# A hybrid decoder layer in one kernel: gate columns evacuated later, four reordered starts, and the keys of the recurrence turned by VectorE from stored squares

## What is computed

```python
xn = rms_norm(x, g_norm);  proj = xn @ w_in
(q, k, v, o_pre, z_ml, i_pre, f_pre, b_g, c_g, xc, z_cv, q_x, z_x) = split_in(proj)
# mLSTM, 4 heads of 256, chunk by chunk (shortened: F, m_t, w_inter, w_C, w_s from the gates)
S = einsum('bthd,bshd->bhts', qb, kb) * exp(Dm - m_t)
num = w_inter * einsum('bthd,bhde->bhte', qb, C) + einsum('bhts,bshe->bhte', S, vb)
C_new = w_C * C + einsum('bhs,bshd,bshe->bhde', w_s, kb, vb)
y_ml = head_norm(sigmoid(o_pre) * num / den) * silu(z_ml)
y_cv = b_g * conv3(c_g * xc) * silu(z_cv)
y_xa = softmax(q_x @ mem_k / sqrt(128)) @ mem_v * silu(z_x)
y = concat([y_ml, y_cv, y_xa]) @ w_out;  out = rms_norm(x + y, g_final)
```

## Time and profile before

| | |
|---|---|
| three runs | 2092.15, 2092.35, 2095.11 us, median 2092.35 |
| the profiled execution | 2096.34 us, its span 2094.5 us |
| PE busy | 2058.3 us, 98% of the span |
| DVE, ACT, POOL busy | 67%, 44%, 42% |
| granted clock of TensorE, mean | 0.992 |
| moved by DMA | 312.00 MB, mean 149 GB/s |

### The profile page before, as it was taken

How to read it: one execution, slowest core, us unless ns; L and a number is a source line. 1 busy time by engine, 2 the same in 40 slices (tenths; PEclk the granted TensorE clock), 3 DMA queues, 4 the chain that set the end, 5 groups by cost and what they waited for, 6 DMA issues and landing times.

```text
span 2094.5 us, 34395 instructions
## 1 busy us (share of the span) xinstructions
PE 2058.3 (98%) x12463; PEld 1914.8 (91%) x12463; DVE 1401.5 (67%) x2189; ACT 928.2 (44%) x1900; POOL 884.0 (42%) x728
## 2 busy tenths in 40 slices
PE   8899999999999999999999999999999999999998
PEld 5899999999999999999999999988887878888886
DVE  7567776698767766797777766643435457667774
ACT  5454445545444455454454455433334323333331
POOL 2455555575555555665555555411000122222220
PEclk9999999999999999999999999999999999999999
DMA  6544334555443345455434465565437577777755
GB/s 217 126 125 126 120 112 132 137 129 130 134 120 114 123 139 139 110 139 128 126 115 126 123 133 148 153 203 184 134 111 212 175 217 205 205 206 210 209 155 112
DMA packets 449768, 312.00 MB, mean 149 GB/s; under 512 B 182976, under 2 KB 414272, under 8 KB 449600
## 3 DMA queue, kind: packets, MB, share of 16 engines
q1 hardware_dynamic: 443920, 291.05, 49.8%
q10 hardware_dynamic: 3376, 10.36, 1.3%
q0 software_dynamic: 2304, 8.39, 1.1%
HBM read 224.82 MB, written 84.92 MB: 148 GB/s over the span
## 4 chain that ended last, share of the span: by engine, by line
PE 93%; SPq 2%; DVE 1%; DMA 1%; issue 1%; ACT 1%; ACTq 0%; DVEq 0%; POOLq 0%; POOL 0%
PE bank L695 20%; PE bank L697 20%; PE bank L696 20%; PE bank L2236 3%; PE bank L2238 3%; PE bank L2237 3%; PE bank L2203 3%; PE bank L2190 2%; PE bank L1649 1%; PE bank L1651 1%; PE bank L1650 1%; PE bank L1661 1%; PE bank L763 1%; PE bank L1663 1%; PE bank L1662 1%
## 5 line engine op out<-in xcount | busy, mean ns | idle before, releaser
L695 PE MATMUL bank<-xh,wh 128*128 128x352 f32 x2688 | 870.8, 324 | 9.4 <-ACT snap L878 8.0
L697 PE MATMUL bank<-xh,wl 128*128 128x352 f32 x2688 | 865.2, 322 | 0.0
L696 PE MATMUL bank<-xl,wh 128*128 128x352 f32 x2688 | 863.4, 321 | 0.0
L1081 DVE TENSOR_TENSOR wl<-raw,wh 128x512 fp32r<-128x512 f32 x384 | 421.8, 1100 | 202.5 <-ACT wh L843 201.4
L695 PEld LDWEIGHTS bank<-xh,wh 128*128 128x128 f32 x2688 | 505.0, 188 | 13.3 <-ACT snap L878 8.9
L696 PEld LDWEIGHTS bank<-xl,wh 128*128 128x128 f32 x2688 | 506.5, 188 | 0.3 <-issue 0.2
L697 PEld LDWEIGHTS bank<-xh,wl 128*128 128x128 f32 x2688 | 506.5, 188 | 0.0
L878 ACT ACTIVATE snap<-bank 128x352 f32<-128x352 f32 x384 | 178.4, 465 | 377.1 <-PE bank L697 377.0
L1081 DVE TENSOR_TENSOR wl<-wt,wh 128x512 fp32r<-128x512 f32 x288 | 236.2, 824 | 115.2 <-ACT wh L843 114.4
L843 ACT ACTIVATE wh<-raw 128x512 fp32r<-128x512 f32 x384 | 240.4, 628 | 156.3 <-PE bank L697 154.8
L643 POOL TENSOR_TENSOR stage<-snap 128x352 f32<-128x352 f32 x96 | 96.4, 1004 | 462.0 <-ACT snap L878 460.8
(11 more groups left out here) (339 smaller groups left out, 2641.7 us busy)
## 6 DMA issues: line engine op xcount, KB each, us to landing
raw<-in_w_in SPq DMA_DIRECT2D x72, 1024.0 KB, 5.5
raw<-in_w_in SPq DMA_DIRECT2D x48, 512.0 KB, 5.5
scr_qk<-stage SPq DMA_DIRECT2D x48, 352.0 KB, 6.2
raw<-scr_qk SPq DMA_DIRECT2D x16, 1024.0 KB, 7.3
area<-scr_vob SPq DMA_DIRECT2D x32, 512.0 KB, 7.1
scr_vob<-stage SPq DMA_DIRECT2D x128, 88.0 KB, 3.2
scr_z<-stage SPq DMA_DIRECT2D x24, 352.0 KB, 2.2
scr_xa<-stage SPq DMA_DIRECT2D x24, 352.0 KB, 2.5
```

Of the source, the lines that this page charges most:

```text
L695: pe.matmul(out, wh[:, b, k, :], xh[:, b, k, :], start=(first and k == 0), stop=False, skip_group_check=True)
L696: pe.matmul(out, wh[:, b, k, :], xl[:, b, k, :], start=False, stop=False, skip_group_check=True)
L697: m = pe.matmul(out, wl[:, b, k, :], xh[:, b, k, :], start=False, stop=(k == 3), skip_group_check=True)
L1081: dve.tensor_tensor(low, source(q, b), high.bitcast(F32), ALU.subtract).then_inc(S["w_low"], 1)
```

## The change

Five edits.

1. **Gate columns.** The evacuation of `bank[6]` leaves its place between two `w_high` and becomes `gates_back(q)`, behind all seven `w_high` of the next job. The four stores to `scr_gate` move from ACT's queue to SP's.
2. **Start of attend.** `out_conv(0)` is cut into its two column halves. PE does half 0, `turn_p(0)`, `scores(1)`, then half 1, `weigh_values(0)`.
3. **q and k of tiles 0 and 1.** Their two loads move from t = 10 to t = 14 of attend.
4. **Start of recur.** `values` is divided into `values` (v) and `out_gates` (o). v and the keys of tile 2 are loaded before `load_unit(1)`, o and `gf` behind it.
5. **Keys.** The four k jobs of a pass also store their rows as squares (eight more DMAs a job). From tile 2 on, SP loads these squares (`key_squares`, 512 KB a tile) into a new tile `kb`, VectorE turns them in one instruction 128x1024 (`turn_keys` of VectorE, in front of update 7 of the tile before), and ACT scales them in place. `kw` has two buffers. PE turns keys only for tiles 0 and 1.

```diff
 def store_parts(s, kind, i):
+    if kind == "qk":
+        return 1 if i < 4 else 5
...
         def store(q):
...
+            if JOBS[q][1] == "gate":
+                s = JOBS[q][0]
+                sp.wait_ge(S["gate_evacuated"], s + 1)
+                for j in range(4):
...
+                    sp.dma_start(w["gate"][...], gst[32 * j:32 * j + 8, :]).then_inc(S["gate_out"], 16)
+                return
...
+                if kind == "qk" and JOBS[q][2] >= 4:
+                    store_squares(sp, q, n, S[f"stored{p}{n}"])
...
+        def gates_back(q):
+            s, kind, _ = JOBS[q]
+            if kind == "gate":
+                act.wait_ge(S["gates_summed"], s + 1)
+                wait(act, S["post"], CN.posted[q][0])
+                if s == 0:
+                    act.wait_ge(S["kv_stored"], 80)
+                    act.wait_ge(S["bif_loaded"], 32)
+                act.activation(gst, bank[6][:, 0:HALF], ACT.Identity, bias=bif[:, 0:1]).then_inc(S["gate_evacuated"], 1)
...
-            if t == WM_FIRST:
+            if t == WM_FIRST + KM // 2:
...
-        out_conv(0)
+        out_conv(0, (0,))
...
         turn_p(0)
         scores(1)
+        out_conv(0, (1,))
...
+        def key_squares(t):
+            if SQUARES_FROM <= t < NT:
+                wait(sp, S["keys_turned"], t - SQUARES_FROM)
+                load_squares(sp, w, 2, kb[:, :], t, S["kb_loaded"])
...
             if t:
                 values(t + 2)
+                key_squares(t + 2)
+                out_gates(t + 2)
...
         def scores(t):
             p = t % 2
             wait(pe, S["C_updated"], updates_before(t))
+            if t >= 2:
+                pe.wait_ge(S[f"qk_loaded{p}"], 16 * (t // 2))
...
+                if d == 0:
+                    pe.wait_ge(S["kw_ready"], 4 * t + h + 1)
+                m = pe.matmul(out, kw[t % 2][:, h, d * P:(d + 1) * P], v1[t % 2][:, h, :], start=True, stop=True)
...
             if t + 1 < NT:
-                turn_keys(t + 1)
+                if t + 1 < SQUARES_FROM:
+                    turn_keys(t + 1)
                 scores(t + 1)
...
+            if t >= SQUARES_FROM:
+                act.wait_ge(S["keys_turned"], t - SQUARES_FROM + 1)
+                for h in range(H):
+                    act.activation(kw[t % 2][:, h, :], kw[t % 2][:, h, :], ACT.Copy, scale=wsc[:, h, t:t + 1]).then_inc(S["kw_ready"], 1)
+                return
...
+        def turn_keys(t):
+            if not SQUARES_FROM <= t < NT:
+                return
+            dve.wait_ge(S["kb_loaded"], 16 * (t - SQUARES_FROM + 1))
+            dve.wait_ge(S["dC_summed"], updates_before(t - 2) + 8)
+            dve.transpose(kw[t % 2], kb[:, :].rearrange("p (h d) -> p h d", h=H)).then_inc(S["keys_turned"], 1)
...
                 update(t, j)
                 if j in (1, 3):
                     turn_v(t + 1, j // 2)
+                if j == 6:
+                    turn_keys(t + 1)
```

More of the change, by code:

```diff
@@ L270, in __init__ @@
             for n in stored_rows(kind):
-                stores[p][n] += 16 * store_parts(s, kind)
+                stores[p][n] += 16 * store_parts(s, kind, i)
             self.posted.append(tuple(posts))
@@ L402, in store_squares @@
         s, kind, i = JOBS[q]
-        f, made = 2 * i + n, stage[:, CN.pair[q] % 2, n, :]
+        f, made = 2 * (i % 4) + n, stage[:, CN.pair[q] % 2, n, :]
         groups = (min(T, PASS * (s + 1)) - PASS * s) // SQ
-        to = w["vob"][int(kind == "o"), PASS // SQ * s:PASS // SQ * s + groups]
+        to = w["vob"][("v", "o", "qk").index(kind), PASS // SQ * s:PASS // SQ * s + groups]
         for b in range(4):
@@ L408, in store_squares @@
                          made[SQ * b:SQ * (b + 1), 0:SQ * groups].rearrange("p (g j) -> p g j", j=SQ)).then_inc(sem, 16)
-        if s == PASSES - 1:
+        if s == PASSES - 1 and kind != "qk":
             sp.dma_start(w["vo"][8 * (kind == "o") + f], made[:, SQ * groups:PASS]).then_inc(sem, 16)
@@ L470, in store @@
         def store(q):
-            if q < 0 or JOBS[q][1] == "gate":
+            if q < 0:
+                return
[3 more added lines that the diff above has]
+                for j in range(4):
+                    at = PASS * s + HALF * (j // 2)
+                    sp.dma_start(w["gate"][8 * (j % 2):8 * (j % 2) + 8, at:at + HALF],
+                                 gst[32 * j:32 * j + 8, :]).then_inc(S["gate_out"], 16)
                 return
@@ L853, in evacuate @@
         def evacuate(q, i):
-            s, kind, _ = JOBS[q]
-            if kind == "gate":
-                if i == 2:
-                    act.wait_ge(S["gates_summed"], s + 1)
-                    wait(act, S["post"], CN.posted[q][0])
-                    if s == 0:
-                        act.wait_ge(S["kv_stored"], 80)
-                        act.wait_ge(S["bif_loaded"], 32)
-                    act.activation(gst, bank[6][:, 0:HALF], ACT.Identity, bias=bif[:, 0:1]).then_inc(S["gate_evacuated"], 1)
-                    act.wait_ge(S["gate_evacuated"], s + 1)
-                    for j in range(4):
-                        at = PASS * s + HALF * (j // 2)
-                        act.dma_start(w["gate"][8 * (j % 2):8 * (j % 2) + 8, at:at + HALF],
-                                      gst[32 * j:32 * j + 8, :]).then_inc(S["gate_out"], 16)
+            if JOBS[q][1] == "gate":
                 return
@@ L1640, in turn_k, with out_conv @@
             s_turned[0] += 1
-        def out_conv(t):
+        def out_conv(t, halves=(0, 1)):
             pe.wait_ge(S["cv_split"], t + 1)
             for k in range(4):
-                for n in range(2):
+                for n in halves:
                     if k == 0:
@@ L1651, in out_conv @@
                     m = pe.matmul(out, yl[:, k, :], wxh[k][:, c], start=False, stop=False)
-            m.then_inc(S["cv_used"], 1)
+            if halves[-1]:
+                m.then_inc(S["cv_used"], 1)
         def out_xa(t):
@@ L1922, in recur @@
     UNIT_LOADS = 12
+    SQUARES_FROM = 2
     qk = qk_tiles(raw)
@@ L1927, in recur @@
     qs = wide[:, 1024:2048].rearrange("p (f t) -> p f t", f=8)
-    kw = wide[:, 2048:3072].rearrange("p (h d) -> p h d", h=H)
+    kw = [a.rearrange("p (h d) -> p h d", h=H) for a in (wide[:, 2048:3072], overlay(22560, "m_kw1", [P, D])[:, :])]
+    kb = overlay(18464, "m_kb", [P, D])
     C = wide[:, 3072:5128].rearrange("p (h d e) -> p h d e", h=H, d=2)
@@ L2047, in _ @@
         values(1)
+        out_gates(1)
         load_unit(sp, 0, rest=False)
@@ L2050, in _ @@
         early(2)
+        values(2)
         sp.wait_ge(before["out_summed"], LAST_X)
+        key_squares(2)
+        load_unit(sp, 1)
+        out_gates(2)
         sp.dma_start(gf[:, :], row_bcast(g_final, P)).then_inc(S["gf_loaded"], 16)
-        load_unit(sp, 1)
-        values(2)
         sp.wait_ge(before["res_added"], LAST_X)
@@ L2180, in numerators @@
                 pe.wait_ge(S["ones"], 2)
+            if t >= SQUARES_FROM:
+                pe.wait_ge(S["t1_ready"], 4 * t)
+                pe.wait_ge(S["den_ready"], t)
+                wait(pe, S["s_C_updated"], 4 * units_before(t))
             for h in range(H):
                 if h < 2:
-                    pe.wait_ge(S["kw_ready"], 4 * t + 2 * h + 2)
+                    if t < SQUARES_FROM:
+                        pe.wait_ge(S["kw_ready"], 4 * t + 2 * h + 2)
                 else:
@@ L2375, in keys @@
                 return
-            wait(act, S["dC_summed"], updates_before(t - 1) + 8 if t else 0)
+            if t >= SQUARES_FROM:
+                act.wait_ge(S["keys_turned"], t - SQUARES_FROM + 1)
+                for h in range(H):
+                    act.activation(kw[t % 2][:, h, :], kw[t % 2][:, h, :], ACT.Copy, scale=wsc[:, h, t:t + 1]).then_inc(S["kw_ready"], 1)
+                return
+            if t:
+                act.wait_ge(before["out_summed"], LAST_X)
             for h in range(H):
                 act.wait_ge(S["k_turned"], 2 * t + h // 2 + 1)
-                act.activation(kw[:, h, :], bank[1 + h // 2][:, (h % 2) * HD:(h % 2 + 1) * HD], ACT.Copy,
+                act.activation(kw[t % 2][:, h, :], bank[1 + h // 2][:, (h % 2) * HD:(h % 2 + 1) * HD], ACT.Copy,
                                scale=wsc[:, h, t:t + 1]).then_inc(S["kw_ready"], 1)
```

10 lines of the change are left out of this document (5 added, 5 removed).

## The result

| | before | after |
|---|---|---|
| timed, median of 4 runs each | 2093.73 us (2092.15 to 2102.52) | 2069.85 us (2065.59 to 2071.29) |
| profiled execution | 2096.34 | 2071.29 |
| its span | 2094.5 | 2069.5 |
| mean granted clock in it | 0.992 | 0.995 |

The ratio is 0.987, 95% interval 0.9849 to 0.9892: the kernel is faster by 1.3%. The forecast was 2059.3, with a range of 2054 to 2072, so the time is inside and the direction right, but of 33.1 us only 25.0 came between the spans of the profiled executions (2094.5 - 2069.5) and 23.9 between the medians. The range held the result by its upper end only: to the forecast alone the prediction gave 2055 to 2066, and the end at 2072 was there for its rival "loads" at 2071.

What follows compares the result with a forecast made beforehand. PE, busy 98% of the span, was taken as the bound, so only PE work and waits count. Terms -8.9 + 1.4 - 5.3 - 6.4 - 13.9 = -33.1 from the median 2092.35 gave 2059.3 us, range 2054 to 2072.

Steps and rivals of the forecast that it cites:

- Gate columns: Gate jobs of project: PE's waits behind ACT's snaps fall from 8.0 to 0.8 us and 1.7 of clock goes, 8.9 less.
- Start of attend: First tiles of attend: ACT's rounding of tile 1's convolution comes later, so PE's wait grows, 1.4 us more.
- q and k of tiles 0 and 1: Tile 11 of attend: weight block issued earlier, 2.4 us of PE's wait and 2.9 of clock gained, 5.3 less.
- Start of recur: First tiles of recur: v no longer late, 4.0 us of PE's wait and 2.4 of clock go, 6.4 less.
- Keys: Recur: PE's eight key transposes vanish from 14 of 16 tiles, 0.99 us a tile, 13.9 us less.
- rival "loads": Moved loads make others late, so attend's and recur's start edits give nothing; 21.4 us gained, 2071; chance 0.14.
- 1.4 us later: Attend's start: half 1 of the convolution ends at 1379.8, 1.4 us later than ACT's rounding at 1378.43.
- SP reaches the block some 2.6 us earlier: Late in attend: without the two q and k transfers SP gets to the weight block some 2.6 us earlier.
- With the same 6.1 us to land: Weight block late in attend: with 6.1 us from issue to use as before, PE's wait falls to 1.6 to 1.8.
- Stores and loads of squares at nothing: Project and recur: eight more DMAs in each of 12 jobs and the key loads were priced at nothing.
- The rival of the slower side: Recur: key squares come late and PE's scores wait in 14 tiles; at 3 us a tile 2101; chance 0.05.
- VectorE as the path: Recur: key turn or wait for scores' weights becomes the path in half the tiles; 26.1 gained, 2066; chance 0.07.

Runs made afterwards that it cites:

- Run 9: Changed kernel with the gate bank evacuated in its old place, between the second and third conversion, stores kept on SP; 2073.0 us, ratio 0.9898.
- Run 2: Changed kernel with out_conv(0) whole again at attend's start; 2067.49 us, ratio 0.9864.
- run 3: Changed kernel with the softmax of tile 1 ahead of its convolution's rounding and low part, in ACT's and VectorE's order; 2060.57 us, ratio 0.9836.
- run 10: Changed kernel with v and keys of tile 2 loaded behind the second sample unit and the final norm's gain; 2073.09 us, ratio 0.9896.
- Run 4: Changed kernel with the last stage's weight blocks loaded ahead of the tile's z and convolution loads on SP; 2064.44 us, ratio 0.985.
- run 6: Changed kernel with the keys of all tiles turned by PE as before, the stores of key squares kept; 2078.21 us, ratio 0.9916.
- Run 7: Changed kernel with keys of all tiles turned by PE and no stores of key squares in the projection; 2081.24 us, ratio 0.9926.
- run 11: Changed kernel with a second 512 KB load of key squares in each of 14 tiles, VectorE waiting for both; 2066.58 us, ratio 0.9867.
- run 8: Changed kernel with VectorE's turn of the keys made twice in each of 14 tiles; 2069.36 us, ratio 0.9871.
- run 1: The changed kernel itself, unedited, profiled and timed again; median 2067.9 us, ratio 0.9865.

## Why the prediction held, and where it was off

**Gate columns, right in size, with half of the cause unseen.** The numbers came out in each part: 0.83 left of 5.40, the clock up, and the two other passes freed (1.7 and 1.6 us shorter for 2.6 forecast). The mechanism did not in one: the prediction put the whole gain down to the place in ACT's order and priced the stores only where they went, on SP's queue. Run 9 has the old place with the stores away from ACT, and keeps the gain of the two later passes and 2.2 us of the first.

**Start of attend, right in mechanism, too small in size.** The step "1.4 us later" is 1.5 in the trace. The place of the wait was not as forecast: the one for the turned weights grew to 4.5 only, not to between 5 and 6, and the rest is the new wait of 1.1 for the queries. What I left out is the clock, whose window fell from 0.81 to 0.65, another 1.2 us. That much belongs to this execution: behind the same wait four of nine executions lost only 0.2 to 0.3 us more than before. Run 2 takes the edit back and gains 1.8 us at its place, run 3 shows what it was lacking.

**q and k of tiles 0 and 1, one step not kept in most executions.** "SP reaches the block some 2.6 us earlier" came out. "With the same 6.1 us to land" failed: it took 8.3 us in the changed kernel, and 7.7 and 7.0 to the use in runs 2 and 3. So of the 2.4 us of waiting 0.5 came, and of the lower clock's 2.9 us 1.2. In run 10 the step held and with it the whole 5.3. So the term is right where the transfer lands in 6 us, and in nine of ten executions it landed later. This is the case "loads" of my rivals in the small: I had put it at both places, and it came at one, in part. What makes the block land after 6.2 or after 8.2 us in the same program no run settles. Run 4 shows that it lands after 3.9 us and that the wait goes when it is queued ahead of z and the convolution's rows. No run takes this edit back, so its 1.7 us is a shift between two profiles and not an experiment.

**Start of recur, right.** -6.0 for -6.4: between the weights of tiles 1 and 2 it is 6.5, and 0.5 is lost ahead of them, where PE waits for the sample unit's state (1.5 for 1.0 before; 0.9 to 1.3 in the other runs). Run 10 gives back 5.9 alone with the order.

**Keys, right in mechanism, mis-sized.** The term 0.99 us a tile was read between two weight loads. These run ahead of the matmuls by different lengths, and PE's own distance is 0.87, which gives 12.2. Measured are 12.5 and, in run 6, 12. So the term was too large by 0.12 us a tile, 1.7 in all. The Trainium skill's 390 ns for a bf16 transpose on TensorE ("VectorE: DVE Perf Modes", "The three transpose paths") would have made 44 us of it. The trace has 0.11 us each in a filled queue. The Trainium skill's advice for TensorE ("VectorE: DVE Perf Modes", "Rules for kernel authors") did not hold here, where VectorE has idle time and PE none: run 6 goes back to it and is 12 us longer in recur.

**Stores and loads of squares at nothing, right.** Run 7 and run 11. The Trainium skill's rule on runs below 512 bytes ("DMA: Bandwidth & Descriptors", "Specifications") shows in no time here: project takes 1287.53 us with these stores and without them. The rival of the slower side needed 2.4 us a tile; twice the bytes gave 0.0.

**VectorE as the path, excluded** by run 8: a second turn of 1.24 us in every tile costs nothing.

**Not priced: the projection's jobs.** They gave back 1.9 us of the gates' gain; this is the next section. And I carried the whole sum to a median, where the profiled execution's place among the runs is worth up to 6 us by itself: it lay 4.0 us above the median before the change and 1.4 after. Of the 10.6 us between forecast and median 8.1 are in the sum and 2.6 in this step.

**Luck in the total.** The median, 2069.85, lies nearer to the rival "loads" (2071) than to the forecast (2059.3). The parts tell them apart: gates, recur's start and keys came, and of that rival only a piece of one place. But 6.7 of the shortfall of 8.1 us lie outside what the sum could see: the changed lengths of project's jobs (1.9) and the clock behind attend's first wait (1.2), which no rival had, and a transfer that landed in time in one execution of ten (3.6).

## What to carry to other kernels

Price work removed from a full engine between the starts of its own instructions and not of its weight loads, and price a wait together with the clock behind it, as a range: behind the same wait of 4.5 us it cost 1.7 us in some executions and up to 2.6 in others. Before splitting work so that another engine may start early, look at what stands ahead in that engine's queue: here the split lost time until the softmax stood first. A load that is issued 2.6 us earlier can land only 0.5 earlier, so move the one that is waited for ahead of its neighbours and not only away from a big one. And an edit that changes two things, here a place in an order and the queue of some stores, is priced as two.

## What was not expected of the hardware

The jobs of project, 84 matmuls 128x352 each, take 13.35, 13.44 or 13.53 us, and PE is busy all the time. The same length holds for three jobs to more than ten, and changes at a longer job in between. ACT's first snaps of two jobs 14 apart in the third pass, in the kernel before:

```profile
1009.30 0.47 ACT L878 ACTIVATE snap<-bank 128x352 f32<-128x352 f32 x1 [1.22 <-PE bank L697]
...
1196.27 0.46 ACT L878 ACTIVATE snap<-bank 128x352 f32<-128x352 f32 x1 [1.33 <-PE bank L697]
```

after the change:

```profile
999.79 0.47 ACT L877 ACTIVATE snap<-bank 128x352 f32<-128x352 f32 x1 [1.23 <-PE bank L709]
...
1188.08 0.47 ACT L877 ACTIVATE snap<-bank 128x352 f32<-128x352 f32 x1 [1.36 <-PE bank L709]
```

and in run 10, whose project is the same program as the changed kernel's:

```profile
999.27 0.47 ACT L877 ACTIVATE snap<-bank 128x352 f32<-128x352 f32 x1 [1.22 <-PE bank L709]
...
1186.24 0.47 ACT L877 ACTIVATE snap<-bank 128x352 f32<-128x352 f32 x1 [1.33 <-PE bank L709]
```

186.97, 188.29 and 186.97 us for 14 jobs, with no lower clock in the third pass. In the changed kernel and in run 1 the lengths repeat job for job, but for the first gate job. In run 10, with the same instructions in project, 47 of 74 jobs that have one of the three lengths have the shortest, in the changed kernel 26 of 73. In run 9, where the gate wait is back, the third pass has 13.35 nearly throughout and the first mostly 13.53. So it is neither the stores of the squares (run 7) nor the program alone. That it follows from how PE came out of an earlier wait is my guess and is not shown; what sets it stays open. It moves the time by 2 us and more, which is as much as some of the edits here.
